# Packing the input projections of a hybrid attention block: 29 output tiles per layer in place of 33

## The chip, the cores and the metric

The kernel runs on one core of one Trainium2 chip. The metric is the device time of one execution in microseconds (us). The program is one launch: two layers of a first model block and then two layers of a second one. Only the first block is touched by the change.

## The reference

A sequence of 512 tokens of width 1024 goes through the first block. Each of its two layers does this:

```python
h = rmsnorm(x, norm1_g[l]) * (1 + sc1) + sh1            # sc1, sh1 from cond @ ada_w[l]
proj = h @ w_in[l] + b_in[l]                            # 1024 -> 6733 columns
qa, ka, va, qi, ki, wi, qkv_b, qkv_c, f_c, gate_logits = split(proj)
# A: 6 heads, rope, keys picked by an index (8 index heads qi, one key ki, weights wi, top 128)
# B: 5 heads, band attention with a relative bias
# C: 5 heads, causal attention with F = cumsum(log_sigmoid(f_c)), f_c: 5 columns, one per head
y = sum(sigmoid(gate_i) * (o_i @ w_branch_i) for i in A, B, C)
x = x + g1 * (y @ w_out[l])
x = x + g2 * swiglu(rmsnorm(x, norm2_g[l]) * (1 + sc2) + sh2)
```

A head has 64 columns. A's queries, keys and values are 384 columns each (6 heads), B's and C's are 320 columns each (5 heads), the index queries 512, the index key 64 and its weights 8. The second block (512 tokens and 256 of context, differential attention, a squared-relu MLP) follows and is computed as before.

## The kernel before

**Data.** Everything is kept transposed: 128 features on the partitions, 512 tokens along a row. A projection makes one output tile of 128 columns of `w_in` by 512 tokens in one PSUM bank. TensorE works in a rounded type, so weights and inputs are split into a high and a low part, and each product is three matmuls: hi x hi, hi x lo, lo x hi (`product`, L560 to L564). An output tile has 8 products along the 1024 rows of h. One product of three matmuls is called a step here, and a tile is 8 steps, 24 matmuls.

**The tiles of a layer before.** The 33 tiles of `TILES` (L43) are: A's queries, keys and values, 3 each; index queries, 4; index key with the index weights, 1; B's and C's queries, keys and values, 3 each, where the third holds only the fifth head in its first 64 rows and 64 columns that nothing reads; and one tile "f" (`OF`), of which 5 columns are read. Together with 24 gate tiles they make up the projection.

**Weights.** SyncE brings them in slabs of 256 or 128 columns (1024 or 512 KB) in the order of `slab_order` (L204), into a ring of 3 raw buffers. A raw buffer is loaded again once it was used. GpSimd splits each slab into hi and lo (L504, L507), two halves per slab, into a ring of 2 split buffers; a split buffer is free once TensorE has finished its slab. Slabs of `ada_w` (the conditioning) lie between them in the same raw ring and go to TensorE without a split (L544).

**Stages of a layer.** norm1; `index` (index queries and key, then index scores with 3 tiles of A's queries woven in); `top` (L744), in which VectorE searches the top 128 keys of each row, 16 rounds, and TensorE meanwhile makes tiles; `attend` for A, B and C (L756); `branches`; output projection; norm2 and the feed-forward part. The tiles that a stage makes beside its own work are listed in `FILL` (L138): 12 in `top` (A's values and keys, B's values and queries), 3 in A (B's keys), 10 in B (C's values, f, queries, keys), 6 gate tiles in C. In `top` the six rope swaps of A's queries and keys (matmuls with a permutation, L631) are put at two places in each of B's three query tiles; VectorE finishes each (L1836 to L1841), after its search.

**Attention.** A unit is one head and one block of 128 query rows, 4 blocks per head: 24 units in A, 20 in B and in C. There is one slot per unit and two more. In slot u TensorE does, in this order: scores of unit u+1 (L778, L780), the fill steps of this slot, the transposition of the probabilities of unit u-1 (L793), the values of unit u-2 (L803), at some slots 16 small matmuls for the conditioning (L544). `pace` (L187) spreads the fill steps evenly: after slot i, `(i+1)*total//slots` of them are done. VectorE does in slot u: the maximum of unit u (L1970, L1977), what the fill asks of it, the normalisation of unit u-1 (L1985, L1987), and, behind the fourth unit of a head, the low part of the head's output (L1995). ScalarE does the exponentials (L1332), PSUM copies (L1340), the outputs' high part (L1347).

**The forget logits.** z is moved out of tile f; `FORGET_AT` (L145) says at which fill tile (at its fifth step) each part is done: `absolute` (VectorE L1926), `log` (ScalarE, L1283 to L1285), `sum` (VectorE, L1930 and the scan L1933), `columns`. The instructions stand in the engine's program between those of the attention, so they delay what stands behind them.

Of the kernel before, what the change touches and what calls it, by code (L numbers as in the profile page):

```python
# [9 lines left out]
F32R = mybir.dt.float32r  # L10
# [5 lines left out]
P = 128  # L16
# [26 lines left out]
TILES = ([OQA + P * i for i in range(6)] + [OQI + P * i for i in range(4)] + [OKI]  # L43
         + [o + P * i for o in (OB, OB + WB, OC, OC + WC) for i in range(3)] + [OF]
         + [o + P * i for o in (OVA, OB + 2 * WB, OC + 2 * WC) for i in range(3)])
TA0, TQI, TKI, TB0, TC0, TF, TV0 = 0, 6, 10, 11, 17, 23, 24
# [18 lines left out]
COLUMN0 = {"A": (OVA, OQA, OKA), "B": (OB + 2 * WB, OB, OB + WB), "C": (OC + 2 * WC, OC, OC + WC)}  # L65
TILE0 = {"A": TA0, "B": TB0, "C": TC0}
OUT0 = {"A": 0, "B": 3, "C": 6}
BRANCH_ROWS = [P, P, P, P, P, HD, P, P, HD]
# [58 lines left out]
def ada_rounds(group):  # L127
# [55 lines left out]
def fill_key(l, kind, which, c):  # L183
    return (l, "gate", 0, c // 2, c % 2) if kind == "gate" else (l, "f") if which == "f" else (l, kind, which, c)
# [19 lines left out]
def slab_order(a):  # L204
# [15 lines left out]
    for l in range(DEPTH):  # L220
        wi = a["w_in"][l]
        def part(kind, which, p):
            o = COLUMN0[kind]["vqk".index(which)]
            matrix((l, kind, which, p), wi, o + 256 * p, 2 * P if not p or (kind, which) == ("C", "v") else P)
# [5 lines left out]
        matrix((l, "qi", 0), wi, OQI, 256)  # L230
        matrix((l, "ki"), wi, OKI, P)
        ada(("norm1", l))
        matrix((l, "qi", 1), wi, OQI + 256, 256)
# [21 lines left out]
        part("C", "q", 1)  # L255
        part("C", "k", 0)
        ada_some("B", 4, 6)
        part("C", "k", 1)
        ada_some("B", 6, 8)
        for jj in range(KT // 2):  # L260
            for br in range(3):
                matrix((l, "gate", jj, br), wi, OG + br * D + jj * 256, 256)
            for br in range(3):
                order.append(((l, "branch", jj, br), 3, 256,
                              [(slice(n, n + 1), slice(0, 256), rows,
                                a["w_branch"][l][r0:r0 + rows, jj * 256:jj * 256 + 256].rearrange("(k p) c -> p k c", k=1))
                               for n, (r0, rows) in enumerate(zip(BRANCH_START[3 * br:3 * br + 3],
                                                                  BRANCH_ROWS[3 * br:3 * br + 3]))]))
# [46 lines left out]
def program(nc, counts, a):  # L315
# [28 lines left out]
    pcol = one.take("layer_columns", [P, 2 * KT + len(TILES) + 3 * KT])  # L344
# [16 lines left out]
    oh = mix.take("o_hi", [P, 9, T], F32R)  # L361
    ol = mix.take("o_lo", [P, 9, T], F32R)
    q_b = Map(nc, mix.at - 2 * 9 * 4 * T + 6 * 4 * T).take("q_b", [P, 3, T])
    k_b = Map(nc, mix.at - 3 * 4 * T).take("k_b", [P, 3, T])
# [50 lines left out]
    bt = pcol[:, 2 * KT:2 * KT + len(TILES)]  # L415
    bg = pcol[:, 2 * KT + len(TILES):]
    z, F = (frow[0:HC, n, :] for n in range(2))
# [32 lines left out]
    def queries(kind, t):  # L450
        return q_b[:, t, :] if kind == "B" else qk[:, t, :]

    def keys(kind, t):
        return k_b[:, t, :] if kind == "B" else qk[:, 3 + t, :]
# [1997 lines left out]
```

## Time and profile before

| | us |
|---|---|
| median of 3 runs | 3659.71 (3658.06 to 3659.78) |
| profiled execution, its own time | 3658.79 |
| its span on the core | 3657.3 |
| TensorE matmuls busy | 3456.6 (95%) |
| VectorE, ScalarE, GpSimd busy | 1333.4, 798.7, 1606.9 |
| DMA, mean | 96 GB/s |

Times in the rows are us from the start of the span unless marked ns. The first layer's `top` runs from 134.0 to 219.95, A to 289.85, B to 389.67, C to about 445; the second layer's `top` from 1122.0 to 1208.48, A to 1278.35, B to 1378.18. A share of busy time is an average over stages with different limits, and busy spans of consecutive matmuls overlap: the distance between two starts is what one costs.

### The profile page before, as it was taken

The numbers are of one execution on the slowest core, as the hardware profiler recorded it, in microseconds if no ns is written. First come the engines' busy times: TensorE is split into PE (matmuls) and PEld (weight loads), VectorE is DVE, ScalarE is ACT, GpSimd is POOL, SyncE is SP. The second block draws the span as 40 slices with busy tenths as digits, with TensorE's granted clock in tenths as the row PEclk, the third lists the DMA queues.
The fourth block names the chain that finished last, engine by engine and source line by source line (L and its number), as shares of the span: only waits on it lengthen the run. The fifth ranks groups of instructions, "written<-read, shape, count | busy, mean of one in ns | idle before, by whom it ended". The sixth has DMA issues, their size and how long they took to land.

```text
span 3657.3 us, 42990 instructions
## 1 busy us (share of the span) xinstructions
PE 3456.6 (95%) x17644; PEld 2721.0 (74%) x17656; DVE 1333.4 (36%) x2287; ACT 798.7 (22%) x1611; POOL 1606.9 (44%) x1020
## 2 busy tenths in 40 slices
PE   5999999999999999999999699889999989889998
PEld 3767777788877677777778587678888878667886
DVE  5843312311157433133111655651211255551113
ACT  2234411100012434111000334420100123421111
POOL 2433266566654223664566332134333333235564
PEclk7999999999999999999999899999999999999999
DMA  6344123333233441234452211022423321113321
GB/s 205 104 135 136 58 81 110 109 92 92 84 107 103 142 147 47 81 103 138 138 150 84 77 47 35 15 88 85 150 93 115 104 58 49 43 50 128 100 95 58
DMA packets 409612, 351.03 MB, mean 96 GB/s; under 512 B 9797, under 2 KB 406853, under 8 KB 409418
## 3 DMA queue, kind: packets, MB, share of 16 engines
q1 hardware_dynamic: 401568, 340.82, 30.0%
q10 hardware_dynamic: 7850, 7.47, 0.8%
q8 instruction: 141, 2.31, 0.3%
q14 instruction: 53, 0.43, 0.0%
HBM read 346.16 MB, written 2.10 MB: 95 GB/s over the span
## 4 chain that ended last, share of the span: by engine, by line
PE 88%; DVE 6%; ACT 3%; issue 1%; DMA 1%; POOL 0%; ACTq 0%; DVEq 0%; POOLq 0%
PE psum L562 26%; PE psum L563 25%; PE psum L564 25%; PE psum L544 2%; PE psum L803 2%; PE psum L911 1%; PE psum L940 1%; DVE psum L1765 1%; PE psum L793 1%; PE psum L739 1%; PE psum L631 1%; DVE k L2245 1%; PE psum L782 1%; PE psum L780 1%; PE psum L778 1%
## 5 line engine op out<-in xcount | busy, mean ns | idle before, releaser
L504 POOL TENSOR_SCALAR weights_hi<-raw_weights 128x1024 fp32r<-128x1024 f32 (+3 forms) x508 | 508.4, 1001 | 1978.6 <-PE psum L564 1745.7
L562 PE MATMUL psum<-h_hi,weights_hi 128*128 128x512 f32 (+1 forms) x2896 | 1170.0, 404 | 68.8 <-DVE h_lo L1789 53.8
L507 POOL TENSOR_TENSOR weights_lo<-raw_weights,weights_hi 128x1024 fp32r<-128x1024 f32 (+3 forms) x508 | 1107.3, 2180 | 42.4
L563 PE MATMUL psum<-h_lo,weights_hi 128*128 128x512 f32 (+1 forms) x2896 | 1101.3, 380 | 0.0
L564 PE MATMUL psum<-h_hi,weights_lo 128*128 128x512 f32 (+1 forms) x2896 | 1100.4, 380 | 0.0
L562 PEld LDWEIGHTS psum<-h_hi,weights_hi 128*128 128x128 f32 x2896 | 551.1, 190 | 232.3 <-issue 111.8
L563 PEld LDWEIGHTS psum<-h_lo,weights_hi 128*128 128x128 f32 x2896 | 552.0, 191 | 118.5 <-issue 16.8
L564 PEld LDWEIGHTS psum<-h_hi,weights_lo 128*128 128x128 f32 x2896 | 550.2, 190 | 112.9
L562 PE MATMUL psum<-hidden_hi,weights_hi 128*128 128x512 f32 (+1 forms) x1120 | 413.6, 369 | 0.0
L564 PE MATMUL psum<-hidden_hi,weights_lo 128*128 128x512 f32 (+1 forms) x1120 | 413.4, 369 | 0.0
L563 PE MATMUL psum<-hidden_lo,weights_hi 128*128 128x512 f32 (+1 forms) x1120 | 413.3, 369 | 0.0
L2045 DVE SCALAR_TENSOR_TENSOR x<-psum,mod,x 128x512 f32<-128x512 f32 (+1 forms) x184 | 123.3, 690 | 582.7 <-PE psum L564 582.5
L562 PEld LDWEIGHTS psum<-hidden_hi,weights_hi 128*128 128x128 f32 x1120 | 210.6, 188 | 40.1 <-issue 1.2
L564 PEld LDWEIGHTS psum<-hidden_hi,weights_lo 128*128 128x128 f32 x1120 | 210.8, 188 | 38.8
L563 PEld LDWEIGHTS psum<-hidden_lo,weights_hi 128*128 128x128 f32 x1120 | 210.6, 188 | 39.0
L1535 ACT ACTIVATE relu_squared<-psum 128x256 f32<-128x256 f32 (+1 forms) x96 | 47.1, 525 | 661.4 <-PE psum L564 661.4
L2158 DVE TENSOR_TENSOR psum<-psum,relu_squared 128x256 f32<-128x256 f32 (+1 forms) x96 | 58.2, 609 | 324.3 <-ACT relu_squared L1535 322.7
L544 PE MATMUL psum<-raw_weights,cond 128*32 128x256 f32 x1536 | 108.7, 405 | 25.8 <-DMA raw_weights<-in_ada_w 14.2
L1428 ACT ACTIVATE silu<-psum 128x512 f32<-128x512 f32 x44 | 26.3, 598 | 375.9 <-PE psum L564 375.9
L2059 DVE TENSOR_TENSOR silu<-psum,silu 128x512 f32<-128x512 f32 x44 | 30.4, 692 | 201.3 <-ACT silu L1428 201.3
L544 PEld LDWEIGHTS psum<-raw_weights,cond 128*32 128x32 f32 x1536 | 42.2, 113 | 76.9 <-issue 37.7
L1195 ACT ACTIVATE squares<-x 128x512 f32<-128x512 f32 x88 | 47.4, 568 | 236.1 <-DVE x L2045 216.8
(262 smaller groups left out, 3606.7 us busy)
## 6 DMA issues: line engine op xcount, KB each, us to landing
raw_weights<-in_ada_w SPq DMA_DIRECT2D x96, 1024.0 KB, 5.2
raw_weights<-in_w_mlp SPq DMA_DIRECT2D x64, 1024.0 KB, 5.4
raw_weights<-in_w_in SPq DMA_DIRECT2D x56, 1024.0 KB, 5.2
raw_weights<-in_w_ffn_in SPq DMA_DIRECT2D x88, 512.0 KB, 5.2
raw_weights<-in_w_in SPq DMA_DIRECT2D x34, 512.0 KB, 4.3
raw_weights<-in_w_out SPq DMA_DIRECT2D x16, 1024.0 KB, 5.2
raw_weights<-in_w_ffn_out SPq DMA_DIRECT2D x16, 1024.0 KB, 5.3
raw_weights<-in_w_branch SPq DMA_DIRECT2D x56, 128.0 KB, 2.2
```

The lines of the kernel that those rows point to most:

```text
L504: gpsimd.tensor_scalar(whi[:, r, c0:c1], raw[:, raw_slot, c0:c1], 1.0, 1.0, ALU.mult, ALU.mult).then_inc(*split_hi.up(*key, half))
L507: gpsimd.tensor_tensor(wlo[:, r, c0:c1], raw[:, raw_slot, c0:c1], whi[:, r, c0:c1].bitcast(F32), ALU.subtract).then_inc(*split.up(*key, half))
L544: ins = tensor.matmul(bank[bk][32 * g:32 * g + 32, 0:256], cond[:, 4 * kk + g, at:at + 32], view[:, 4 * kk + g, :], start=c == 0 and kk == ...
L562: tensor.matmul(out, sh, mh, start=first, stop=False, skip_group_check=shared)
L563: tensor.matmul(out, sh, ml, start=False, stop=False, skip_group_check=shared)
L564: return tensor.matmul(out, sl, mh, start=False, stop=last, skip_group_check=shared)
L631: tensor.matmul(bank[bk][:, 0:n], matrix, x, start=True, stop=True).then_inc(*swapped.up(*key))
L803: ins = tensor.matmul(bank[3][:, i * P:i * P + P], values_of(kind, h // 2)[:, j, :], probt[:, q, j * P:j * P + P], start=j == 0, stop=j == i)
L1195: scalar.activation(part_of(work, 1 + (k + 1) % 2 if k else 0, x0, x1), X[:, k, x0:x1], ACT.Square).then_inc(*squared.up(which, l, s, k))
L1535: scalar.activation(sq2[:, count % 2, 0:c1 - c0], bank[bk][:, 0:c1 - c0], ACT.Relu).then_inc(*moved.up(L, "relu2", chunk, n, s))
L2045: vector.scalar_tensor_tensor(out=xs, in0=bank[bk][:, at:at + x1 - x0], scalar=mod[:, part * 8 + n, m:m + 1], in1=xs, op0=ALU.mult, op1=AL ...
L2158: vector.tensor_tensor(x, x, sq2[:, count % 2, 0:c1 - c0], ALU.mult).then_inc(*dve_misc.up(L, "square", count))
```

## The change

The fifth heads of B and C share tiles, and the forget logits share the tile of the index key. The host orders the columns of `w_in` and `b_in` anew (`packed_columns`), with zero columns where a tile is padded. A layer has 29 tiles: B's queries, keys and values take 2 tiles each (heads 0 to 3); C's third tile holds head 4 of B in its lower and head 4 of C in its upper half; the tile of the index key holds at columns 64 to 68 the forget logits and at 96 to 103 the index weights. B's third head tile is then read out of C's buffers, and C's fifth head goes first, since it must be in the upper half. The loads of the third B tiles fall away; C's tile 2 is loaded and made before C's tiles 0 and 1. The outputs of the two fifth heads share tile 5. ScalarE has one more small move per layer, of z, right behind the index key.

```diff
 FILL = {"index": [("A", "q", c) for c in range(3)],
-        "top": ([("A", which, c) for which in "vk" for c in range(3)] + [("B", which, c) for which in "vq" for c in range(3)]),
-        "A": [("B", "k", c) for c in range(3)],
-        "B": ([("C", "v", c) for c in range(3)] + [("C", "f", 0)] + [("C", "q", c) for c in range(3)]
-              + [("C", "k", 0), ("C", "fcol", 0), ("C", "k", 1), ("C", "k", 2)]),
+        "top": ([("A", which, c) for which in "vk" for c in range(3)] + [("B", which, c) for which in "vq" for c in range(2)]),
+        "A": [("B", "k", c) for c in range(2)],
+        "B": ([("C", "v", c) for c in range(3)] + [("C", "q", 2), ("C", "k", 2), ("C", "q", 0), ("C", "q", 1), ("C", "k", 0),
+                                                  ("C", "fcol", 0), ("C", "k", 1)]),
         "C": [("gate", "", g) for g in range(6)]}
-FORGET_AT = {("q", 0): "absolute", ("q", 1): "log", ("q", 2): "sum", ("k", 1): "columns"}
+FORGET_AT = {("v", 2): "absolute", ("q", 2): "log", ("k", 2): "sum", ("k", 1): "columns"}
+HEAD_ORDER = {"A": tuple(range(HA)), "B": tuple(range(HB)), "C": (4, 0, 1, 2, 3)}
+BRANCH = (((0, 0, P), (1, 0, P), (2, 0, P)), ((3, 0, P), (4, 0, P), (5, 0, HD)), ((6, 0, P), (7, 0, P), (5, HD, HD)))
...
         # slab_order
-        for which in "vq":
-            part("B", which, 0)
-            part("B", which, 1)
+        part("B", "v", 0)
+        part("B", "q", 0)
         part("B", "k", 0)
-        ada_some("A", 0, 4)
-        part("B", "k", 1)
-        ada_some("A", 4, 8)
+        ada_some("A", 0, 8)
         part("C", "v", 0)
         part("C", "v", 1)
         ada_some("B", 0, 2)
+        part("C", "q", 1)
+        part("C", "k", 1)
+        ada_some("B", 2, 4)
         part("C", "q", 0)
-        ada_some("B", 2, 4)
-        part("C", "q", 1)
-        part("C", "k", 0)
         ada_some("B", 4, 6)
-        part("C", "k", 1)
+        part("C", "k", 0)
         ada_some("B", 6, 8)
...
         # top, TensorE
-                    if (kind, which) == ("B", "q") and k in (1, 5):
+                    if (kind, which) == ("B", "q") and k in (0, 3, 6):
...
         # index, ScalarE
             scalar.activation(ki, bank[2][:, :], ACT.Identity, bias=bt[:, TKI:TKI + 1]).then_inc(*moved.up(l, "ki"))
+            scalar.activation(z, bank[2][heads_c, :], ACT.Identity, bias=bt[heads_c, TKI:TKI + 1]).then_inc(*moved.up(l, "f"))
...
         # index, TensorE
-            free[2] = moved.at(l, "ki")
+            free[2] = moved.at(l, "f")
...
         # attend, TensorE, values
                 if i == 0:
                     tensor.wait_ge(*free[3])
+                    if (kind, h) == ("B", 4):
+                        tensor.wait_ge(*moved.at(l, "C", "vt", 2))
...
         # lay_out, on the host
+    for o in (OB, OB + WB, OB + 2 * WB):
+        cols += heads(o, range(4))
+    for o in (0, WC, 2 * WC):
+        cols += heads(OC + o, range(4)) + head(OB + o, 4) + head(OC + o, 4)
```

## Rows read from the trace of the kernel before

**Rows 1.** The page: busy time by engine, and the chain that ended last.

```profile
PE 3456.6 (95%) x17644; PEld 2721.0 (74%) x17656; DVE 1333.4 (36%) x2287; ACT 798.7 (22%) x1611; POOL 1606.9 (44%) x1020
...
PE 88%; DVE 6%; ACT 3%; issue 1%; DMA 1%; POOL 0%; ACTq 0%; DVEq 0%; POOLq 0%
```

**Rows 2.** Busy time by stage: top, A, B; then A of layer two.

```profile
core 0: us, PE busy (x) PEld busy (x) DVE busy (x) ACT busy (x) POOL busy (x), PEclk, DMA share, GB/s
...
134.00:219.95 85.95, 81.31 (x389) 60.71 (x388) 63.26 (x172) 12.58 (x21) 43.15 (x32) 0.98 0.38 117
219.95:289.85 69.90, 63.26 (x450) 47.01 (x456) 28.94 (x82) 33.66 (x89) 12.60 (x10) 1.00 0.51 161
289.85:389.67 99.82, 96.76 (x583) 74.02 (x583) 33.35 (x108) 37.72 (x88) 35.07 (x25) 1.00 0.45 139
...
1208.48:1278.35 69.87, 63.26 (x450) 46.99 (x457) 28.90 (x82) 33.65 (x89) 12.61 (x10) 1.00 0.51 161
```

**Rows 3.** Instructions in time order, TensorE, `top`: start, duration, line, count.

```profile
145.37 0.40 PE L562 MATMUL psum<-h_hi,weights_hi 128*128 128x512 f32 x1
...
146.07 0.39 PE L562 MATMUL psum<-h_hi,weights_hi 128*128 128x512 f32 x1
...
147.47 0.60 PE L669 MATMUL psum<-constants,softmax_buffers 128*128 128x128 f32 x4
147.83 0.48 PE L562 MATMUL psum<-h_hi,weights_hi 128*128 128x512 f32 x1
```

**Rows 4.** The same view, end of `top`: swap, VectorE's rope, first scores.

```profile
197.51 1.02 PE L631 MATMUL psum<-qk,constants 128*128 128x512 f32 x2
...
198.57 0.70 DVE L1836 TENSOR_TENSOR psum<-psum,rope_sin 128x512 f32<-128x512 f32 x1 [13.91 <-PE psum L631]
...
219.95 0.23 PE L777 MATMUL psum<-select_mask,identity_bf 128*128 128x128 bf16 x1 [1.28 <-ACT softmax_buffers L1361]
```

**Rows 5.** The same view, a wait in `top` and the steps behind it.

```profile
175.02 0.75 PE L562 MATMUL psum<-h_hi,weights_hi 128*128 128x512 f32 x1 [2.32 <-POOL weights_lo L507]
...
176.43 0.63 PE L562 MATMUL psum<-h_hi,weights_hi 128*128 128x512 f32 x1
...
177.71 0.63 PE L562 MATMUL psum<-h_hi,weights_hi 128*128 128x512 f32 x1
```

**Rows 6.** The same view, stage A: TensorE's waits, and VectorE before them.

```profile
236.53 1.14 DVE L1987 TENSOR_SCALAR softmax_buffers<-softmax_buffers,softmax_stats 128x256 f32<-128x256 f32 x1
...
249.42 0.35 DVE L1987 TENSOR_SCALAR softmax_buffers<-softmax_buffers,softmax_stats 128x256 f32<-128x256 f32 x1
...
237.72 0.44 PE L793 MATMUL psum<-constants,softmax_buffers 128*128 128x128 f32 x2 [1.32 <-DVE softmax_buffers L1987]
...
249.83 0.44 PE L793 MATMUL psum<-constants,softmax_buffers 128*128 128x128 f32 x2 [0.80 <-DVE softmax_buffers L1987]
...
271.45 0.44 PE L793 MATMUL psum<-constants,softmax_buffers 128*128 128x128 f32 x2 [1.02 <-DVE softmax_buffers L1987]
```

**Rows 7.** The same view, stage B: the forget sum and what waits for it.

```profile
353.50 2.40 POOL L507 TENSOR_TENSOR weights_lo<-raw_weights,weights_hi 128x1024 fp32r<-128x1024 f32 x1
...
336.70 0.67 DVE L1926 SCALAR_TENSOR_TENSOR forget<-forget 5x512 f32<-5x512 f32 x1
...
353.64 2.80 DVE L1930 SCALAR_TENSOR_TENSOR forget<-forget 5x512 f32<-5x512 f32 x1
356.48 1.21 DVE L1933 TENSOR_TENSOR_SCAN forget<-small,forget 5x512 f32<-5x512 f32 x1
...
358.19 0.44 PE L793 MATMUL psum<-constants,softmax_buffers 128*128 128x128 f32 x2 [1.42 <-DVE softmax_buffers L1987]
```

**Rows 8.** The same view, stage B, slot 11: VectorE's maximum, TensorE's scores and transposition.

```profile
338.46 0.70 DVE L1977 CUSTOM_DVE_ANT_0 psum<-psum,softmax_buffers 128x512 f32<-128x512 f32 x1
...
338.67 0.39 PE L780 MATMUL psum<-k_b,softmax_buffers 128*128 128x128 f32 x2
...
341.70 0.49 PE L793 MATMUL psum<-constants,softmax_buffers 128*128 128x128 f32 x3
```

More of the change, by code:

```diff
@@ L41 @@
 FFN = -(-8 * D // 768) * 256
[L43 to L46, printed above, removed]
+TILE_OF = {("A", "q"): 0, ("A", "k"): 3, ("A", "v"): 6, ("B", "q"): 14, ("B", "k"): 16, ("B", "v"): 18,
+           ("C", "q"): 20, ("C", "k"): 23, ("C", "v"): 26}
+TQI, TKI, NT = 9, 13, 29
+FCOL, WICOL = HD, 96
 REL = 128
@@ L183, in fill_key, with half_of, out_tile, tile_kind @@
 def fill_key(l, kind, which, c):
-    return (l, "gate", 0, c // 2, c % 2) if kind == "gate" else (l, "f") if which == "f" else (l, kind, which, c)
+    return (l, "gate", 0, c // 2, c % 2) if kind == "gate" else (l, kind, which, c)
+def half_of(kind, h):
+    return 1 if (kind, h) == ("C", 4) else h % 2
+def out_tile(kind, h):
+    return 5 if h == 4 and kind != "A" else {"A": 0, "B": 3, "C": 6}[kind] + h // 2
+def tile_kind(kind, t):
+    return "C" if (kind, t) == ("B", 2) else kind
 def pace(steps, total, slots):
@@ L222, in part @@
         def part(kind, which, p):
-            o = COLUMN0[kind]["vqk".index(which)]
-            matrix((l, kind, which, p), wi, o + 256 * p, 2 * P if not p or (kind, which) == ("C", "v") else P)
+            matrix((l, kind, which, p), wi, TILE_OF[kind, which] * P + 256 * p, P if p else 256)
         def ada_some(group, j0, j1):
@@ L485, in sync_engine @@
             for ks, cs, rows, src in pieces:
-                sync.dma_start(view[0:rows, ks, cs], src).then_inc(*arrived[r].up(*key))
+                p0, p1 = rows if isinstance(rows, tuple) else (0, rows)
+                sync.dma_start(view[p0:p1, ks, cs], src).then_inc(*arrived[r].up(*key))
         out = a["out"].rearrange("(k p) t -> k p t", p=P)
@@ L638, in tile1 @@
                 slab_key, at, first, last = (l, "gate", 0, c // 2), c % 2 * P, c % 2 == 0, c % 2 == 1
-            elif which == "f":
-                slab_key, at, first, last = (l, "C", "v", 1), HD, False, True
             else:
                 slab_key, at, first, last = (l, kind, which, c // 2), c % 2 * P, c % 2 == 0, c > 0
-                if (kind, which, c) == ("C", "v", 2):
-                    last = False
             if first:
@@ L757, in attend @@
             heads = HEADS[kind]
-            units = [(h, i) for h in range(heads) for i in range(TT)]
+            units = [(h, i) for h in HEAD_ORDER[kind] for i in range(TT)]
             def scores(u):
@@ L806, in values @@
                 if i == TT - 1:
-                    free[3] = o_lo.at(l, kind, h // 2, h % 2)
+                    free[3] = o_lo.at(l, kind, h)
             steps = ada_steps(kind, l) if kind != "C" else iter(())
@@ L1309, in attend @@
             heads = HEADS[kind]
-            units = [(h, i) for h in range(heads) for i in range(TT)]
+            units = [(h, i) for h in HEAD_ORDER[kind] for i in range(TT)]
             def bias(u):
@@ L1951, in attend @@
             heads = HEADS[kind]
-            units = [(h, i) for h in range(heads) for i in range(TT)]
+            units = [(h, i) for h in HEAD_ORDER[kind] for i in range(TT)]
             def prepare(h):
```

141 lines of the change are left out of this document (78 added, 63 removed).

## The prediction, made before the changed kernel was built or run

> **What bounds the kernel now.** I read the page first, then the busy time by stage, then the instructions in time order around each place that the diff touches. The reader is to see in [rows 1] that TensorE is busy 95% of the span and makes 88% of the chain that ended last: whatever shortens TensorE's own program shortens the kernel, unless something else is late just there. [rows 2] ask that question for the three stages that lose tiles. In `top` TensorE is busy 81.3 of 85.95 us, in A 63.26 of 69.90, in B 96.76 of 99.82. So `top` and B are bound by TensorE nearly throughout, and A has 6.6 us of waits: there, part of what is removed may only uncover a wait. The last line of [rows 2] is A in the second layer, 0.03 us from the first layer's, so I work out one layer and double it.
>
> **Price of a tile.** In [rows 3] two consecutive steps start at 145.37 and 146.07, 0.70 us apart (three matmuls, 0.233 each, the clock at its upper level, 2.4 GHz). A tile of 8 steps is 5.6 us. A value tile has four transpositions more, from 147.47 to 147.83, 0.36 us. 8 tiles go in both layers, 192 matmuls: 44.8 us is what the change takes from TensorE's program, 45.5 with the transpositions. The rest is to find what of it comes back.
>
> **`top`: two tiles, B's third values and third queries.** 11.2 us, and 0.36 for the transpositions. The cover to look at is VectorE's search. In [rows 4] its first rope starts at 198.57 after 13.91 us of idling, and waits for TensorE's swap at 197.51. One value tile fewer ahead of it and the swap one step earlier bring the swap to 197.51 - 5.6 - 0.36 - 0.7 = 190.85, while VectorE is free from 198.57 - 13.91 = 184.66: 6.2 us of slack are left, no wait. The six swaps now stand three and two steps apart where they stood four. A swap and the product behind it cost 0.86 more than plain steps, so they come every 2.96 us, once 2.26; a rope is about 2.1 us of VectorE, so it keeps up. The last swap stands one step nearer the end of the stage, and ScalarE's copies before A's first scores (1.28 us idle, [rows 4]) come after the same work as before. VectorE may be behind A's first maximum by 0 to 0.9 us; I take 0.2. The wait of 2.32 us in [rows 5] lies ahead of B's first value slab, which still stands in the raw ring behind the same conditioning slab, so it stays, with its 8 slow matmuls. B's query slab now comes right behind it, and is needed at 175.0 + 11.8 = 186.8; its split runs behind that of the value slab, 7 us, and is half done by about 182. `top` gives 11.2 + 0.36 - 0.2 = 11.35.
>
> **A: one tile, 8 steps.** `pace` gave 24 steps to 26 slots, a step in all but slots 0 and 13. 16 steps leave out 0, 2, 5, 7, 10, 13, 15, 18, 20, 23. TensorE waits in slots 6, 10 and 18 [rows 6]: there the transposition waits for a normalisation that stands behind the low part of the previous head's output in VectorE's program, and that chain starts with TensorE's values one slot earlier. What TensorE does meanwhile is cover, and a step less there only lengthens the wait. Two of the eight lost steps are such (slots 10 and 18: 0.80 becomes 1.50, 1.02 becomes 1.72). In slots 2, 5, 7, 15, 20 and 23 the normalisation is there 0.7 us or more ahead, so they count fully: 6 x 0.70 = 4.2 us. Further, in slot 6 the normalisation took 1.14 us against 0.35 in slot 10 [rows 6], while GpSimd split the slab of B's third keys; that slab is gone, and 1.32 us of wait should become 0.80: 0.5 more. A gives 4.7, between 3.5 (two more steps are cover) and 6.1 (all count, and the 0.5).
>
> **B: one tile, the forget tile.** 8 steps of 81, 5.6 us, spread over slots that wait nowhere but one: in slot 14 the forget sum (2.80 and 1.21 us) stands on VectorE ahead of a normalisation, and TensorE waits 1.42 us [rows 7]. The order of the fill moves the parts. With 73 steps in 22 slots, the sum is asked for at step 36, in slot 11. It stands there behind the maximum of unit 11 and ahead of the normalisation of unit 10. In [rows 8] that maximum starts at 338.46; it now comes 0.67 earlier, as `absolute` (336.70, [rows 7]) leaves slot 10 for slot 6: it ends with its accumulator at 338.5. The sum takes 4.0 us, normalisation 0.6: TensorE can transpose at 343.1. TensorE is there after scores at 338.67 - 0.70 and 3.03 - 0.70 us of work: 340.3. That is a wait of 2.8 us if the first operation takes 2.80, and 0.7 if it takes the 0.67 of its sister [rows 7]. [rows 7] show why it took 2.80: GpSimd's TENSOR_TENSOR ran from 353.50 to 355.90, and the operation, started at 353.64, ended 0.54 us behind it. In the new order C's first query slab is split from about 333.5, when the split buffer comes free, to 340.5; its second TENSOR_TENSOR (338.1 to 340.5) meets the sum again, but later in its run, since slot 9 has one step more now. I take 1.95 us of wait for 1.42: 0.5 lost, with ends of 0.7 gained and 1.5 lost. B gives 5.6 - 0.5 = 5.1; C's v slab, now half as wide, may shorten the splits at B's start that slow VectorE there; I leave that at 0.
>
> The Trainium skill (GPSIMD Engine Reference, 1. Specifications) says that GpSimd shares its SBUF interfaces with VectorE, and that VectorE's instructions with two SBUF inputs, or in a two-port mode, contend. Here the trace agrees: 2.80 us beside a GpSimd operation. By the rule the sum is cheap in any slot in which GpSimd rests, and the change would give 1.1 us per layer more than I count if slot 11 were such.
>
> **Moved and added, at nothing.** The move of z (5 rows, about 0.6 us of ScalarE) stands behind the move of the index key, while TensorE does 24 matmuls of the next tile, 5.6 us; without that cover it would delay the second of the index query tiles, 0.6 us per layer. The new wait for C's values ahead of B's head 4 falls in slot 18, and those values are made by step 24, slot 7. B's head 4 wants C's query tile 2 in slot 13 (made by step 32, slot 9) and key tile 2 in slot 15 (step 40, slot 12). C's query slab 0 can be loaded once C's third key slab is split, about slot 8, lands 5.3 us later and is needed at step 40, slot 12, near 343: with the split's first half, 3.5 us, it is some 6 us early. The conditioning slabs of B that stand behind it come just in time at worst: 0, or 1 us. C has the same 48 fill steps; its heads only change places, the branch products keep their number and widths. Three slabs per layer fewer free GpSimd and the DMA, which bound nothing.
>
> **Sum.** Per layer 11.35 + 4.7 + 5.1 = 21.15; two layers 42.3. From the profiled execution's 3658.79 us that is 3616.5; it lies 0.9 below the median of the three runs, 3659.71, so the forecast is 3617 us.
>
> **Rivals.** (a) The fill of the attention stages is cover altogether, and only `top` gives: 2 x 11.35 = 22.7, 3637 us. For it: A's 6.6 us of waits all lie on a chain through VectorE and ScalarE. Against: in B TensorE waits 3 us in 100 [rows 2], so its tile can't be cover. 5%. (b) The longer waits let the clock fall. The granted clock over A is 1.00 [rows 2] with waits up to 1.32 us; behind the 2.32 us of [rows 5] steps start 1.28 apart (176.43, 177.71), the 1.2 GHz level, for 8 matmuls, 1.5 us. A wait of 2 to 2.8 us behind the sum is of that size. Once per layer, with 1 us more of wait: 2 x 2.5 = 5, 3622 us. 20%. (c) The other side: with a third of its fill gone, A runs at the lower level from end to end in both layers. Steps at 1.28 for 0.70 make 63.26 us of TensorE's work 115.7; less the 6.6 of waits and more the new ones that is at least 45 us per layer, 90 in all against 42.3 gained, 3707 us. It decides once some 25 us of TensorE's work per layer run at the lower level. Against it: nothing in A before fell at waits of 1.32, and the new ones are at most 1.7. 2%. The Trainium skill (TensorE: Matmul & The Clock Gate, Part 1) has the clock follow how busy TensorE has lately been, which speaks for (b) and (c) in kind; no row has a wait of 1.7 us, so the trace does not say at which it would act. (d) A slab comes late: C's q1 and k1 slabs now stand before two conditioning slabs, and a wait of one load, 5 us, once per layer would give 3627 us. 5%. (e) The change does what it says and every removed step counts: 2 x (11.56 + 6.1 + 6.3) = 47.9, 3612 us. 8%.
>
> **Chances and range.** Forecast 3617 (3614 to 3620) 60%, (b) 20%, (e) 8%, (a) 5%, (d) 5%, (c) 2%. The range 3611 to 3627 holds the forecast, (b), (e) and most of (d). About 0.2%, 7 us, is what a measurement tells from no change: faster 97%, same 1%, slower 2%.
>
> **What would show it.** `top` 74.6 us for 85.95, A 65.2 for 69.90, B 94.7 for 99.82, C within 0.5. 192 matmuls fewer on the lines of the three products. VectorE's first rope after some 6 us of idling, not 13.9. In A no transposition waits 1.3 us in slot 6, and two wait 1.5 to 1.7. In B the one long wait is in slot 11, near 2 us, behind the forget sum. Wrong would be: a stage that shortens by less than 60% of its steps, a wait for a slab or a conditioning load that was not there, a clock share in A or B under 0.97, or any change in C, the branches or the second block beyond 1 us.

## The result, and the profile after

The changed kernel takes 3629.26 us (median of 4 runs, 3626.02 to 3632.27) against 3659.74 (3658.06 to 3661.22) beside it: ratio 0.9914, interval 0.9899 to 0.9928. The gain is 30.5 us where 42.3 were forecast, and the time lies outside the range given. A second set of runs gave 3630.12 (3627.67 to 3632.54), ratio 0.9919 (0.9904 to 0.9933). The profiled execution took 3632.27 us and is the slowest of its four; its span is 26.3 us shorter than before's (3631.0 for 3657.3).

The page after, busy time and the chain that ended last, beside [rows 1]:

```profile
PE 3426.8 (94%) x17456; PEld 2690.6 (74%) x17456; DVE 1337.1 (37%) x2287; ACT 794.5 (22%) x1603; POOL 1579.2 (43%) x996
...
PE 88%; DVE 6%; ACT 3%; DMA 1%; issue 1%; POOL 1%; ACTq 0%; DVEq 0%; SPq 0%; POOLq 0%
```

The matmuls came off as said (188 fewer recorded; on each of the three product lines 2832 for 2896, 64 fewer, so 192). TensorE's busy time fell by 29.8 us. The busy time by stage tells where: top, A and B of layer one, then of layer two (columns as in [rows 2]).

```profile
134.00:209.57 75.57, 70.90 (x342) 52.19 (x342) 68.45 (x174) 11.69 (x20) 35.92 (x24) 0.98 0.42 133
209.57:277.16 67.59, 60.22 (x432) 43.37 (x432) 27.67 (x82) 33.12 (x88) 8.79 (x7) 0.97 0.43 135
277.16:372.76 95.60, 91.28 (x558) 69.48 (x558) 32.30 (x108) 37.28 (x87) 32.28 (x24) 1.00 0.46 145
...
1184.94:1252.53 67.59, 60.21 (x433) 43.22 (x433) 27.69 (x82) 33.11 (x88) 8.80 (x7) 0.97 0.42 135
1252.53:1350.96 98.43, 94.11 (x558) 71.25 (x558) 32.32 (x108) 37.29 (x87) 32.28 (x24) 0.97 0.45 141
```

The last three figures of a line are the granted clock, the DMA share and GB/s. The reader is to see the clock: A had 1.00 in [rows 2] and has 0.97 in both layers; B has 0.97 in layer two. In A, TensorE is busy 3.0 us less, although 5.6 us of matmuls left. From the starts of the stages in the two traces (the last row from the start of VectorE's L1780 at 2096.87 before, the same operation, L1797, at 2068.50 after):

| stage, us | before, layer 1 / 2 | after | gain | forecast |
|---|---|---|---|---|
| index and `top` | 154.3 / 155.3 | 143.7 / 146.7 | 10.6 / 8.6 | 11.35 |
| A | 69.9 / 69.9 | 67.6 / 67.6 | 2.3 / 2.3 | 4.7 |
| B | 99.8 / 99.8 | 95.6 / 98.4 | 4.2 / 1.4 | 5.1 |
| C and branches | 227.2 / 228.8 | 229.4 / 227.8 | -2.2 / 1.0 | 0 |
| second block, most of it | 1560.4 | 1562.5 | -2.1 | 0 |

With 0.3 in the rest these are the 26.3 us. Of the 16 us missing in this execution, 3.5 are in `top`, 4.8 in A, 4.6 in B, 3 behind them.

**A, layer one of the changed kernel**, instructions in time order. Beside [rows 6]: the wait of slot 6 (0.55 at 225.20), of slot 10, of slot 18, and GpSimd and VectorE ahead of the last.

```profile
225.20 0.44 PE L800 MATMUL psum<-constants,softmax_buffers 128*128 128x128 f32 x2 [0.55 <-DVE softmax_buffers L2004]
...
236.64 0.44 PE L800 MATMUL psum<-constants,softmax_buffers 128*128 128x128 f32 x2 [1.50 <-DVE softmax_buffers L2004]
...
255.49 2.34 POOL L516 TENSOR_TENSOR weights_lo<-raw_weights,weights_hi 128x1024 fp32r<-128x1024 f32 x1
...
257.11 0.88 DVE L2004 TENSOR_SCALAR softmax_buffers<-softmax_buffers,softmax_stats 128x256 f32<-128x256 f32 x1
...
258.04 0.44 PE L800 MATMUL psum<-constants,softmax_buffers 128*128 128x128 f32 x2 [2.02 <-DVE softmax_buffers L2004]
258.31 0.39 PE L812 MATMUL psum<-softmax_buffers,values 128*128 128x128 f32 x2
258.63 1.93 PE L553 MATMUL psum<-raw_weights,cond 128*32 128x256 f32 x16
```

Slot 10 waits 1.50 us, as forecast. Slot 18 waits 2.02, forecast 1.72: the normalisation takes 0.88 for 0.35 and ends with GpSimd's operation. Behind it the sixteen conditioning matmuls take 1.93 us where they take 1.07 elsewhere: the clock has gone to its lower level, 1.2 for 2.4 GHz.

**A, layer two.** Here slot 18 waits 2.05 us and its sixteen matmuls take 1.07; the clock fell at the start of the stage instead, behind two short waits that stood in the kernel before too (1.28 us at 219.95 in [rows 4], and 0.72 at 221.72; no slow matmul behind them there).

```profile
1184.94 0.23 PE L784 MATMUL psum<-select_mask,identity_bf 128*128 128x128 bf16 x1 [1.28 <-ACT softmax_buffers L1378]
...
1186.71 0.34 PE L784 MATMUL psum<-select_mask,identity_bf 128*128 128x384 bf16 x1 [0.72 <-ACT softmax_buffers L1347]
...
1188.40 0.63 PE L572 MATMUL psum<-h_lo,weights_hi 128*128 128x512 f32 x1
```

**B, slot 11, layer one**, and the same place in layer two (last three rows). It answers to [rows 7] and [rows 8].

```profile
322.05 2.50 POOL L516 TENSOR_TENSOR weights_lo<-raw_weights,weights_hi 128x1024 fp32r<-128x1024 f32 x1
...
322.23 2.47 DVE L1975 COPY softmax_buffers<-bias_diagonals 128x256 f32<-128x256 f32 x1
...
325.71 0.68 DVE L1947 SCALAR_TENSOR_TENSOR forget<-forget 5x512 f32<-5x512 f32 x1
326.43 1.22 DVE L1950 TENSOR_TENSOR_SCAN forget<-small,forget 5x512 f32<-5x512 f32 x1
...
328.35 0.55 PE L800 MATMUL psum<-constants,softmax_buffers 128*128 128x128 f32 x3 [3.19 <-DVE softmax_buffers L2004]
...
1303.74 0.90 PE L800 MATMUL psum<-constants,softmax_buffers 128*128 128x128 f32 x3 [3.20 <-DVE softmax_buffers L2004]
1304.43 1.06 PE L812 MATMUL psum<-softmax_buffers,x 128*128 128x128 f32 x4
1305.42 1.94 PE L553 MATMUL psum<-raw_weights,cond 128*32 128x256 f32 x16
```

The forget sum costs 1.9 us, uncontended; what GpSimd holds is the copy of the bias diagonals ahead of it, 2.47 us. TensorE waits 3.2 us, for 1.95 forecast. Behind the wait the clock fell in layer two (1.94), not in layer one.

**`top`, layer two of the changed kernel**: GpSimd gets B's value slab late, and TensorE waits for the split.

```profile
1139.84 7.16 SPq L495 DMA_DIRECT2D raw_weights<-in_w_in  x3
...
1147.11 1.04 POOL L513 TENSOR_SCALAR weights_hi<-raw_weights 128x1024 fp32r<-128x1024 f32 x1 [10.21 <-DMA raw_weights<-in_w_in]
...
1150.64 0.80 PE L571 MATMUL psum<-h_hi,weights_hi 128*128 128x512 f32 x1 [4.07 <-POOL weights_lo L516]
```

The slab is issued at 1139.84, with the 1 MB query slab right behind it, and GpSimd starts on it 7.3 us later; before, the slab issued at 1154.66 was split from 1160.02, 5.4 us later, and TensorE waited 2.16 us. In layer one the same two slabs are issued in the same order, the first is split 5.5 us later (172.76 after 167.22), and the wait is 2.35 us, as in [rows 5]. Behind the 4.07 us 12 matmuls run at the lower clock, where it was 7.

### The profile page after: what moved, and what is told of

Same layout as the page of the kernel before. It is cut to its first block, busy times and chain, and to the rows that moved or that the text cites. A ratio compares the mean times of both kernels' runs of the same rounds, so it can differ in the third digit from the quotient of the medians.

```text
span 3631.0 us, 42550 instructions
## 1 busy us (share of the span) xinstructions
PE 3426.8 (94%) x17456; PEld 2690.6 (74%) x17456; DVE 1337.1 (37%) x2287; ACT 794.5 (22%) x1603; POOL 1579.2 (43%) x996
## 4 chain that ended last, share of the span: by engine, by line
PE 88%; DVE 6%; ACT 3%; DMA 1%; issue 1%; POOL 1%; ACTq 0%; DVEq 0%; SPq 0%; POOLq 0%
PE psum L571 25%; PE psum L572 24%; PE psum L573 24%; PE psum L553 2%; PE psum L812 2%; PE psum L927 1%; PE psum L956 1%; DVE psum L1782 1%; PE psum L800 1%; PE psum L744 1%; PE psum L640 1%; PE psum L787 1%; DVE k L2261 1%; DMA raw_weights<-in_ada_w 1%; PE psum L785 1%
## 5 line engine op out<-in xcount | busy, mean ns | idle before, releaser
L513 POOL TENSOR_SCALAR weights_hi<-raw_weights 128x1024 fp32r<-128x1024 f32 (+3 forms) x496 | 500.3, 1009 | 1980.9 <-PE psum L573 1667.0
L571 PE MATMUL psum<-h_hi,weights_hi 128*128 128x512 f32 (+1 forms) x2832 | 1143.4, 404 | 69.6 <-DVE h_lo L1806 51.4
L516 POOL TENSOR_TENSOR weights_lo<-raw_weights,weights_hi 128x1024 fp32r<-128x1024 f32 (+3 forms) x496 | 1088.0, 2194 | 41.4
L572 PE MATMUL psum<-h_lo,weights_hi 128*128 128x512 f32 (+1 forms) x2832 | 1077.8, 381 | 0.0
L573 PE MATMUL psum<-h_hi,weights_lo 128*128 128x512 f32 (+1 forms) x2832 | 1077.0, 380 | 0.0
L571 PEld LDWEIGHTS psum<-h_hi,weights_hi 128*128 128x128 f32 x2832 | 540.5, 191 | 229.9 <-issue 108.7
L572 PEld LDWEIGHTS psum<-h_lo,weights_hi 128*128 128x128 f32 x2832 | 541.2, 191 | 115.7 <-issue 15.9
L573 PEld LDWEIGHTS psum<-h_hi,weights_lo 128*128 128x128 f32 x2832 | 539.1, 190 | 110.5
L1445 ACT ACTIVATE silu<-psum 128x512 f32<-128x512 f32 x44 | 26.3, 598 | 375.2 <-PE psum L573 375.2
```

The lines of the kernel that those rows point to most:

```text
L513: gpsimd.tensor_scalar(whi[:, r, c0:c1], raw[:, raw_slot, c0:c1], 1.0, 1.0, ALU.mult, ALU.mult).then_inc(*split_hi.up(*key, half))
L516: gpsimd.tensor_tensor(wlo[:, r, c0:c1], raw[:, raw_slot, c0:c1], whi[:, r, c0:c1].bitcast(F32), ALU.subtract).then_inc(*split.up(*key, half))
L571: tensor.matmul(out, sh, mh, start=first, stop=False, skip_group_check=shared)
L572: tensor.matmul(out, sh, ml, start=False, stop=False, skip_group_check=shared)
L573: return tensor.matmul(out, sl, mh, start=False, stop=last, skip_group_check=shared)
```

## The experiments

All are the changed kernel with one edit, each with its own runs of the kernel before. W, D and the like are the theories named in the texts on record. Differences below are between medians, against the 3630.12 of the second set of the changed kernel. The granted clock falls at different places in different executions of one kernel, so a difference of medians under some 4 us is read from the rows and not from the times.

**The changed kernel again** (no edit).

> The changed kernel itself, as the partner of the others on the same chip. Theory W (the missing gain is two waits on VectorE, behind the forget sum in slot 11 of B and in slot 18 of A, and the slow matmuls behind them): about 3629 us; the profile again has the wait of 3.2 us in B and of 2.0 us in A in both layers, since they follow from the order of the work. Rival S (the missing gain is scatter of TensorE's clock that has nothing to do with the change): the median comes out nearer 3617 and the places of the slow matmuls differ. Rival D (the second 1 MB slab directly behind B's value slab makes that slab land late, 7.2 us for 5.4 as in layer two): the wait of about 4 us before B's value tiles is there again in at least one layer.

3630.12 us. The waits came again, 3.18 us in B, 2.19 and 1.93 in A's slot 18, 3.78 in `top` of layer two. Theory W holds for the waits and D for layer two. Where the clock fell changed in part: in slot 18 in both layers, at A's start in layer two again, in B in neither. A takes 67.7 and 69.0 us, B 95.6 in both layers. So which wait is followed by slow matmuls is scatter in part, as rival S had it; the median is not.

**The forget sum two slots later.**

```diff
-FORGET_AT = {("v", 2): "absolute", ("q", 2): "log", ("k", 2): "sum", ("k", 1): "columns"}
+FORGET_AT = {("v", 2): "absolute", ("q", 2): "log", ("q", 0): "sum", ("k", 1): "columns"}
```

> Only the place of the forget sum differs: it is done at the fifth step of C's query tile 0, slot 13, in place of C's key tile 2, slot 11. Theory W: the wait in slot 11 of B shrinks from 3.2 us by the sum's 1.9 to 1.3 (VectorE's copy of the bias diagonals, 2.5 us beside GpSimd, stays there), none appears in slot 13, and no slow matmuls behind it in layer two (2.7 us): 2 x 1.9 + 2.7 = 6.5 us less than the changed kernel. If the copy is the whole cause (rival C): nothing changes, 0 us. Rival S: 0 us, scatter only.

3622.32 us (3619.13 to 3627.91), ratio 0.9902 (0.9886 to 0.9919): 7.8 off. Its slowest run, 3627.9, lies within those of the changed kernel; the rows carry the reading. Slot 11 of this kernel:

```profile
320.06 2.47 DVE L1975 COPY softmax_buffers<-bias_diagonals 128x256 f32<-128x256 f32 x1
...
324.03 0.55 PE L800 MATMUL psum<-constants,softmax_buffers 128*128 128x128 f32 x3 [1.02 <-DVE softmax_buffers L2004]
```

The copy is held as before, the sum is gone from the slot, and 2.2 us of the wait with it; B takes 93.5 us in both layers, with no slow matmul.

**A's 16 steps put where TensorE waits.** `pace` spreads them evenly; here a table gives them.

```diff
+STEPS_A = {0: 1, 1: 1, 4: 1, 6: 2, 10: 3, 12: 1, 14: 1, 18: 3, 22: 1, 23: 1, 25: 1}
...
-            fill = pace(fill1(l, kind), fill_steps(kind), len(units) + 2)
+            fill = pace_a(fill1(l, kind)) if kind == "A" else pace(fill1(l, kind), fill_steps(kind), len(units) + 2)
```

> The same 16 fill steps in A, but laid where TensorE waited: 2 in slot 6, 3 each in slots 10 and 18, 1 each in 0, 1, 4, 12, 14, 22, 23, 25. Theory W: A's waits of 0.72, 0.55, 1.50 and 2.02 us go and with them the slow stretch of 1.6 us behind the last: A falls from 67.6 to about 61.5 us in each layer, 12 us less than the changed kernel. Rival P (a fill step in A is worth 0.70 wherever it stands, and A is bound by TensorE's own work): A stays at 67.6, 0 us. If only the clock counts: 2 x 1.6 = 3 us less.

3622.25 us (3618.38 to 3624.11), 0.9896 (0.9881 to 0.9911): 7.9 off, for 12 forecast. A takes 63.4 and 63.3 us for 67.6 (61.5 forecast), and its clock stays up. Slot 18 keeps a wait:

```profile
254.01 2.35 DVE L2017 TENSOR_SCALAR softmax_buffers<-softmax_buffers,softmax_stats 128x256 f32<-128x256 f32 x1
...
256.42 0.44 PE L813 MATMUL psum<-constants,softmax_buffers 128*128 128x128 f32 x2 [1.37 <-DVE softmax_buffers L2017]
```

The normalisation, 0.35 us alone, now meets GpSimd's operation near its start and is held 2.35. B paid a part back: the clock fell behind slot 11 in both layers (98.3 and 97.2 us).

**GpSimd's last subtraction of C's query slab behind the forget sum, then behind the normalisation.** The two runs differ in the signal.

```diff
                 gpsimd.wait_ge(*split_hi.at(*key, half))
+                if key[1:] == ("C", "q", 0) and half:
+                    gpsimd.wait_ge(*dve_misc.at(key[0], "F"))         # first run
+                    gpsimd.wait_ge(*normed.at(key[0], "B", 10))       # second run, in its place
```

> GpSimd's last TENSOR_TENSOR of C's query slab 0 waits until VectorE has the forget sum; all else as in the changed kernel. Theory W with GpSimd's part in it: VectorE's copy in slot 11 takes 0.3 us in place of 2.5, the sum stays there with 1.9: the wait in slot 11 shrinks from 3.2 to about 1.0 us, and with it the slow stretch of layer two: 2 x 2.2 + 2.7 = 7 us less than the changed kernel. If the copy is slow for another reason (not GpSimd): it stays at 2.5 us, 0 us, or more time, since TensorE then waits for the split.

> The changed kernel with GpSimd's last subtraction of C's first query slab held until the normalisation of B's unit 10 is done, so that it runs neither beside VectorE's copy of the bias diagonals nor beside the normalisation. Theory G (VectorE is held 2.2 us by GpSimd in this slot, on top of the 1.9 us of forget operations): the copy takes 0.28 us for 2.47, the normalisation 0.42, TensorE's wait in slot 11 of B falls from 3.2 to about 1.0 us in each layer: 4.4 us off, and up to 2.7 us more where the clock fell behind that wait: 3624 to 3626 us. Rival: the subtraction runs beside the next VectorE operations instead (the normalisation of unit 11) and holds those, wait of over 2 us one slot later, time within 2 us of 3630 us.

Behind the sum: 3627.37 us (3626.47 to 3631.73), 0.9914 (0.9899 to 0.9928), 2.8 off, not to be told from no change; 7 were forecast. The rows of slot 11:

```profile
322.28 0.28 DVE L1977 COPY softmax_buffers<-bias_diagonals 128x256 f32<-128x256 f32 x1
...
325.65 2.34 POOL L518 TENSOR_TENSOR weights_lo<-raw_weights,weights_hi 128x1024 fp32r<-128x1024 f32 x1 [3.63 <-DVE forget L1952]
...
325.73 2.47 DVE L2006 TENSOR_SCALAR softmax_buffers<-softmax_buffers,softmax_stats 128x384 f32<-128x384 f32 x1
...
328.26 0.55 PE L802 MATMUL psum<-constants,softmax_buffers 128*128 128x128 f32 x3 [3.06 <-DVE softmax_buffers L2006]
```

The copy takes 0.28 us, so it was GpSimd that held it; but the delayed operation starts 0.08 us ahead of the normalisation and holds that one instead. Behind the normalisation: 3623.93 us (3619.79 to 3625.98), 0.9901 (0.9888 to 0.9915), 6.2 off, as forecast:

```profile
319.69 0.28 DVE L1977 COPY softmax_buffers<-bias_diagonals 128x256 f32<-128x256 f32 x1
...
323.62 0.55 PE L802 MATMUL psum<-constants,softmax_buffers 128*128 128x128 f32 x3 [1.01 <-DVE softmax_buffers L2006]
...
323.88 2.47 DVE L2006 TENSOR_SCALAR softmax_buffers<-softmax_buffers,softmax_stats 128x512 f32<-128x512 f32 x1
```

The 2.2 us of holding now falls on the normalisation of unit 11, for which nobody waits. B takes 93.4 us in both layers.

**B's value slab earlier.**

```diff
         ada_some("rope", 0, 1)
         part("A", "k", 0)
-        ada_some("rope", 1, 3)
+        ada_some("rope", 1, 2)
         part("A", "k", 1)
-        ada_some("rope", 3, 4)
+        ada_some("rope", 2, 3)
         part("B", "v", 0)
+        ada_some("rope", 3, 4)
```

> The changed kernel with one reordering ahead of A: the projection slab of B's values is issued before the fourth conditioning slab of `rope` and A's last key slab's neighbour moves up with it (order rope 0, A keys, rope 1, A keys, rope 2, B values, rope 3, B queries, B keys). Theory S (TensorE stands at B's values because that 1 MB slab lands late behind the one issued before it, and the clock falls behind that wait): the waits of 2.2 to 2.4 us in layer one and 3.5 to 4.1 us in layer two at the first matmuls of B's values go, and with them the stretches at the lower clock behind them (8 and 12 or 13 matmuls, about 1.6 and 2.5 us): 2.4 + 1.6 + 3.8 + 2.5 = 10 us off, about 3620 us. Rival: the DMA queue is the limit whatever the order, so another slab comes late instead by the same amount: the waits show at another line and the time stays within 2 us of the changed kernel's 3630 us.

3619.80 us (3617.68 to 3621.13), 0.9891 (0.9878 to 0.9905): 10.3 off. Neither layer's `top` has a wait for GpSimd or slow matmuls behind it; index and `top` take 140.1 and 139.8 us for 143.8 and 146.5. Theory S stands.

**One tile back in A.** FILL gives A a third tile, ("B", "x", 0), whose 24 matmuls use B's first key slab and are read by nobody. The edit also holds that slab's split buffer until the added tile is made.

```diff
-        "A": [("B", "k", c) for c in range(2)],
+        "A": [("B", "k", 0), ("B", "k", 1), ("B", "x", 0)],
...
```

> The changed kernel with one tile of 24 matmuls computed once more inside A's fill (as before the change; the result of that tile is thrown away, the output does not change). It tells what a tile in A is worth. The prediction's working counted 4.7 us for it in each layer; A's measured gain was 2.3 us. Theory W (the tile stood partly under TensorE's waits for the softmax, which come back as longer waits when it goes, and the 2.0 us wait in slot 18 brings the lower clock behind it): A goes from 67.6 back to 69.9 us in each layer, +2.3 us each, +4.6 us in all, about 3635 us. Rival (steps at full value, 24 x 0.23 us = 5.6 us each): +11 us, 3641 us.

3634.12 us (3631.91 to 3635.32), 0.9930 (0.9916 to 0.9943): 4.0 more. A of layer one, its waits of slots 10 and 18:

```profile
208.72:277.65 68.93, 63.84 (x457) 47.01 (x457) 27.25 (x82) 33.03 (x88) 8.82 (x7) 1.00 0.42 133
```

```profile
237.81 0.44 PE L805 MATMUL psum<-constants,softmax_buffers 128*128 128x128 f32 x2 [0.80 <-DVE softmax_buffers L2009]
...
259.21 0.44 PE L805 MATMUL psum<-constants,softmax_buffers 128*128 128x128 f32 x2 [0.77 <-DVE softmax_buffers L2009]
```

5.6 us of matmuls lengthen A by 1.3 us: the waits give back 0.7 and 1.25 (of which 0.5 is the normalisation, free of GpSimd here), slot 23's 0.33 goes, and the clock is at 1.00 again, 1.6 us. A at 68.9 for 69.9 forecast: even less came back than theory W said, and the steps at full value are excluded. The 4.6 us forecast for the whole were met for another reason too: the rest is in B, where the clock now fell behind slot 11 in both layers (97.3 and 97.2 us).

**GpSimd's second subtraction of C's value slab behind A's unit 17.**

```diff
                 gpsimd.wait_ge(*split_hi.at(*key, half))
+                if key[1:] == ("C", "v", 0) and half:
+                    gpsimd.wait_ge(*normed.at(key[0], "A", 17))
```

> The changed kernel with GpSimd's second subtraction of C's value slab held until the normalisation of A's unit 17 is done, nothing else. Theory K (the clock falls behind TensorE's wait of about 2 us in A's slot 18 and this costs 1.6 us in the slot behind): the normalisation takes 0.35 us for 0.88, the wait falls from 2.0 to 1.5 us, as long as the one in slot 10 behind which no matmul was slow, the sixteen conditioning matmuls behind it take 1.07 us for 1.93, and A takes 65.5 us for 67.6 in each layer: 4.2 us off, about 3626 us. Rival (the lower clock comes from the few and small matmuls of that stretch, whatever the wait): only the 0.5 us of the wait go in each layer, 3629 us, and the sixteen matmuls still take 1.9 us.

3628.36 us (3625.06 to 3631.46), 0.9914 (0.9900 to 0.9927): 1.8 off by the medians, which the intervals don't tell from nothing; 4.2 were forecast. Slot 18 of A, then slot 11 of B:

```profile
255.53 0.44 PE L802 MATMUL psum<-constants,softmax_buffers 128*128 128x128 f32 x2 [1.50 <-DVE softmax_buffers L2006]
...
256.12 1.07 PE L555 MATMUL psum<-raw_weights,cond 128*32 128x256 f32 x16
...
324.45 0.58 PE L802 MATMUL psum<-constants,softmax_buffers 128*128 128x128 f32 x3 [3.19 <-DVE softmax_buffers L2006]
...
325.81 1.94 PE L555 MATMUL psum<-raw_weights,cond 128*32 128x256 f32 x16
```

In layer one slot 18 does as theory K said: wait 1.50, the sixteen matmuls 1.07 us, A 65.6 us. In layer two its wait is 1.50 too, but A takes 67.2 us for the 65.5 forecast, since the clock fell at the start of the stage, behind the waits of 1.28 and 0.72 us. Slot 18 by itself shows little of what the length does: in the changed kernel 2.05 us there had left the clock up as well. And what A won B lost: the clock fell behind slot 11 in both layers (97.2 and 97.1 us).

**Three edits together** (sum later, A's steps, B's value slab), **and these with both delays of GpSimd.**

> The changed kernel with three edits together: the forget sum two slots later in B, A's fill steps put in the slots where TensorE waits, B's values slab issued earlier. Each takes away a wait of another stage, so the gains should add: 7.8 us (sum later, measured) + 7.9 us (A's steps, measured) + about 8 to 10 us (slab earlier, expected above) = 24 to 26 us off the changed kernel's 3630 us, 3604 to 3606 us. Rival: what is gained in one stage comes back in the next (the DMA queue or the clock), and the sum falls short by more than 5 us: 3610 us or more.

> All three edits of the run with three edits (the sum two slots later, A's steps where A waits, B's values slab earlier) and both delays of GpSimd's subtractions (C's value slab behind A's unit 17, C's query slab behind B's unit 10). What is left there of TensorE's waits behind GpSimd are 1.41 us in A's slot 18 and 1.06 us in B's slot 11 in each layer. Both go or nearly go: 2 x 2.4 = 4.8 us off 3606 us, about 3601 to 3602 us. Rival: the subtraction then holds the next normalisation (unit 18) and TensorE waits one slot later by 0.5 to 1.5 us in A: 3603 to 3606 us.

Three edits: 3606.20 us (3603.12 to 3607.46), 0.9853 (0.9840 to 0.9867), 23.9 off, 0.2 us behind the forecast; the single gains are 7.8 + 7.9 + 10.3 = 26.0. With the delays of GpSimd: 3601.77 us (3600.33 to 3607.77), 0.9846 (0.9832 to 0.9859), as forecast, the best of this study, 28 us under the changed kernel and 58 under the one before. The further 4.4 us have overlapping intervals, but the rows show them: in slots 18 and 11 TensorE has no wait left.

```profile
250.45 0.39 PE L591 MATMUL psum<-h_hi,weights_lo 128*128 128x512 f32 x1
250.68 0.38 PE L818 MATMUL psum<-constants,softmax_buffers 128*128 128x128 f32 x2
...
314.72 0.39 PE L591 MATMUL psum<-h_hi,weights_lo 128*128 128x512 f32 x1
314.96 0.49 PE L818 MATMUL psum<-constants,softmax_buffers 128*128 128x128 f32 x3
```

A takes 62.3 us in both layers, B 92.5 and 92.3.

## Why the prediction was wrong, and where it was right

Three steps of the prediction failed, and all three are waits or their price: the clock was put at nothing, the wait of slot 11 was reckoned without one operation that stands there, and the wait in `top` was said to stay. Of the 16.0 us missing in the profiled execution, the clock in A makes 3.2 and A's waits 1.6; B's wait 1.8 and the clock behind it 2.8; `top` 3.5; some 3 lie behind these stages.

**What held.** The count of matmuls and the price of a step; that one layer's steps come off one by one where nothing waits (in A, slots 2, 5, 7 and 20 lost 0.70 us each, slot 15 0.54); slot 6, 0.55 us of wait for 1.32; slot 10, 1.50. From the wait in `top` to A's start layer one went from 44.93 to 33.28 us, 11.65 for the 11.35 forecast; layer two 10.63. VectorE's rope had 4.5 us of idling ahead of it (some 6 forecast), so it never became the bound. Rival (a), fill as mere cover, is out in B. In A it is partly true: the tile put back costs 2.9 to 3.1 us beside a stage A with the clock up (68.9 for 65.8 and 66.0), so 2.5 to 2.7 of its 5.6 us are cover; another 1.6 are the clock.

**Term A, 4.7 us, measured 2.3.** The sum of the steps was nearly right. 5.6 and 0.5 off, slot 10 back 0.7, slot 18 back 1.0 (0.7 forecast; GpSimd holds the normalisation), slot 23 back 0.33: 4.1. Two stages A of the experiments, unchanged there, in which the clock stayed up took 65.8 and 66.0 us, 4.1 and 3.9 less than before. What failed most is the clock at no cost: 1.6 us per layer, against 0.6 from the waits. That was rival (b), given 20% and placed in B, behind a wait grown to 2 us or more. Only layer one's fall came so. Layer two's came at the start of A, behind two waits that the change left as they were; its being there and not in the kernel before goes by the instant, as told below, and is as much chance as effect.

**Term B, 5.1 us, measured 4.2 and 1.4.** The wait in slot 11 was taken as 1.95 us, in bounds of 0.7 to 2.8, and is 3.2. The prediction asked which of the forget operations would meet GpSimd, and looked only at those. The copy of the bias diagonals that stands there too was left out. The sum itself met no GpSimd operation (0.68 us), and for that case the prediction had 0.7 us of wait; with the copy free, 1.0 was measured. GpSimd's second subtraction was timed to start 0.3 us behind the start of the maximum (338.1 against 338.46 - 0.67); taking the 2.2 us of holding out, it started 0.7 us ahead of it (322.05 against 324.92 - 2.19), and so beside the copy of the bias diagonals. The two delays, 2.2 us of holding and 1.9 us of sum, add up, and TensorE's own work hides about 1 us of them: wait 1.0 with the copy held and no forget sum, 1.0 with the sum and a free copy, 3.2 with both, none with neither. The clock behind it, up to 2.8 us, is again rival (b).

**Term `top`, 11.35 us, measured with the index stage 10.6 and 8.6.** The wait ahead of B's values "stays", it said; in layer two it went from 2.16 to 4.07 us, rival (d) in small. The prediction gave the query slab right behind it no price. While both are under way the DMA moves some 360 GB/s (361 from 1142 to 1147 us), and the first was usable after 5.5 us in layer one and after 7.3 in layer two. That the slab behind it is the cause is not shown: it stands there in layer one as well, and in layer two of the kernel with the tile back in A the first was usable after 5.7 us (split from 1147.63, issued at 1141.97) and the wait was 2.46. Why the layers differ stays open. The run with the slab order changed shows the whole of this place at 10 us, with the wait that stood in the kernel before.

**Rival (b) was the mechanism to weigh most**, and its price differs from what was said: a fall costs 1.6 to 2.8 us, and comes in some layers and not in others. The length of a wait alone does not decide. Behind slot 11 TensorE waited 3.03 to 3.20 us in 14 layers of seven profiled executions; the clock fell behind it in 9 of them. In the other 5 it had fallen in A's slot 18, 70 us earlier, and in none of the 9 had it done so. In slot 18 waits of 1.93 to 2.19 us brought it in some layers and not in others (2.02 at 258.04: sixteen matmuls 1.93 us; 2.05 at 1235.00: 1.07), and no wait of up to 1.50 us there did. At the start of A the 1.28 and 0.72 us brought it in 7 of the 18 stages that have both.

What tells these places apart is the instant. In the traces' record of the granted clock all stretches at the lower level of one execution start at instants that are evenly spaced, without an exception in the twelve profiles. Put the start of each wait between two such instants, 0 at the one and 1 at the next. In slot 11 the nine waits with a fall begin at 0.89 to 0.95 or 0.06 to 0.36, the five without at 0.48 to 0.65. At the start of A the seven with a fall begin at 0.95 to 0.11, the eleven without at 0.22 to 0.93. In slot 18, of the waits of 1.93 us and more, the six with a fall begin at 0.20 to 0.40, the five without at 0.42 to 0.55 or at 0.92. The wait of slot 11 begins a quarter of the spacing further on than that of slot 18, so behind a fall in slot 18 it begins where none comes: that one fall should act on the other is not needed. This was read from the traces afterwards; no run moved a wait for it. Length counts beside it: in slot 18 a wait of 1.50 us that began at 0.26 and one of 1.86 at 0.37 brought no fall.

The instant fits the experiments: whatever changed A's length moved B's wait, and in all six layers in which slot 18's wait was mended and slot 11's left, B paid (97.2 us with slot 18 mended, 97.3 with the tile back, up to 98.3 with A's steps moved), while removing the wait in slot 11 leaves both B stages clean (93.4 to 93.5). So where a wait that long stands, the fall is a matter of luck; with the wait cut to 1.0 us or gone it did not come. The Trainium skill (TensorE: Matmul & The Clock Gate, Part 1) ties the clock to how busy TensorE has lately been, and has this activity watched by a free-running window that the kernel's start does not reset. Both agree in kind: the falls come in attention slots with waits, and at evenly spaced instants.

**GpSimd's hold.** Three VectorE operations with SBUF operands took until GpSimd's TENSOR_TENSOR ended, whatever their own length: copy 0.28 to 2.47 us, normalisation 0.35 to 2.35, another 0.42 to 2.47. The Trainium skill (SBUF — State Buffer, Who interferes with whom) says that VectorE and GpSimd take turns at a shared port pair under an exclusive lock, so the later one is blocked until the earlier ends, and that the two-port modes of VectorE need it too. The runs agree with the lock: each held operation ended within 0.3 us of GpSimd's, and all three have one SBUF tensor as input; that they ran in a two-port mode no row shows. The prediction had put the 1.14 us of a normalisation in A down to GpSimd, but in B it drew on the rule only as contention of the two-input sum.

**The remaining 2 to 3 us** of the profiled execution lie at C's start and in the second block. They are in part the lower clock at other places: at C's start in layer one after (374.7) and not before, in layer two before (1380.0) and not after; in the second block 13 slow matmuls behind the wait that ends at 3249.5, 7 behind the same wait before. They came in some executions and not in others; the rest stays open.

**Sums.** Three small terms of the prediction are off: two more steps of cover in A give 3.3, not 3.5; a wait of 2.8 for 1.42 loses 1.4, not 1.5; and 0.7 for 1.95 would give 1.25 per layer, not 1.1. None moves the forecast.

## What to carry to other kernels

Before a piece of work is taken out beside an attention chain, list for each slot everything that stands in VectorE's program there, not only what the change moves, and lay GpSimd's operations over it: a held operation costs the rest of GpSimd's, and holds add. Count every wait of an attention stage as a clock risk and none as certain: 1.28 and 0.72 us close together brought a fall in 7 of 18 places, 3.2 us in 9 of 14, and the length did not say which. Expect that mending one wait lets the clock fall at the next one; the gains came when all were mended. After a removal, spread what is left anew: the same 16 steps in other slots, the sum two slots later and one slab earlier were worth 24 us together, four fifths as much again as the change itself.

## What was not expected of the hardware

An operation of 0.28 us took 2.47 us beside GpSimd's. Of two 1 MB loads issued one behind the other, the first was usable after 5.5 us in one layer and 7.3 in the other; before, with a 0.5 MB slab behind it, after 5.5 and 5.4. And whether the clock fell behind a 3.2 us wait, in 9 of 14 places, went with the instant at which the wait began, not with its length.
